# Attention remainders of the probabilities: from GpSimd and the vector engine together to the vector engine alone

## The reference, cut to what matters

```python
logits = q @ k.T * scale            # f32
p = softmax(logits, axis=-1)
out = p @ v
```

## Time and profile before

| | us |
|---|---|
| median of three runs (lowest, highest) | 4124.23 (4122.91, 4127.02) |
| span of the profiled execution, the only time the profile gives for itself | 4126.6 |
| attention, start of the first `ph` (line 1449) to start of the last, layer 0 | 388.81 to 932.48 |
| busy: PE, DVE, ACT, POOL | 3858.3, 1950.5, 1620.1, 1416.4 |

### The profile page before, as it was taken

How to read it: one execution, slowest core, us unless ns; L and a number is a source line. 1 busy time by engine, 2 the same in 40 slices (tenths; PEclk the granted TensorE clock), 3 DMA queues, 4 the chain that set the end, 5 groups by cost and what they waited for, 6 DMA issues and landing times. The chain is left out here.

```text
span 4126.6 us, 51789 instructions
## 1 busy us (share of the span) xinstructions
PE 3858.3 (93%) x19141; PEld 3134.3 (76%) x19141; DVE 1950.5 (47%) x2740; ACT 1620.1 (39%) x2581; POOL 1416.4 (34%) x904
## 2 busy tenths in 40 slices
PE   6899999998799999999869999999897999999997
PEld 5687787677588888888657767876675888888885
DVE  4114767871633343334450267678517343334336
ACT  2324767882422212221342357678624211221123
POOL 2223555662432212211432345556515112211224
PEclk8998999999899999999989989999998999999998
DMA  5321220101211111111123212111012111111113
GB/s 172 123 72 60 62 61 23 36 17 63 91 42 41 36 36 41 41 36 36 72 86 124 64 58 74 45 26 30 21 66 94 38 39 41 36 36 41 41 30 128
DMA packets 194303, 234.47 MB, mean 57 GB/s; under 512 B 13759, under 2 KB 157669, under 8 KB 193573
## 3 DMA queue, kind: packets, MB, share of 16 engines
q1 hardware_dynamic: 194125, 232.18, 18.3%
HBM read 178.05 MB, written 58.29 MB: 57 GB/s over the span
## 5 line engine op out<-in xcount | busy, mean ns | idle before, releaser
L211 PE MATMUL ps<-hh,wh 128*128 128x512 f32 (+1 forms) x3264 | 1180.8, 362 | 117.1 <-DVE wl L504 44.9
L212 PE MATMUL ps<-hl,wh 128*128 128x512 f32 (+1 forms) x3264 | 1165.1, 357 | 0.0
L213 PE MATMUL ps<-hh,wl 128*128 128x512 f32 (+1 forms) x3264 | 1162.7, 356 | 0.0
L211 PEld LDWEIGHTS ps<-hh,wh 128*128 128x128 f32 x3264 | 623.6, 191 | 216.6 <-issue 86.5
L1875 POOL TENSOR_TENSOR wl<-raw,wh 128x1024 fp32r<-128x1024 f32 x128 | 306.4, 2401 | 1279.4 <-ACT wh L1804 1279.4
L212 PEld LDWEIGHTS ps<-hl,wh 128*128 128x128 f32 x3264 | 623.6, 191 | 92.5 <-issue 5.7
L213 PEld LDWEIGHTS ps<-hh,wl 128*128 128x128 f32 x3264 | 622.6, 191 | 89.0
L1911 DVE SCALAR_TENSOR_TENSOR cb<-ps,params,cb 128x1023 f32<-128x1023 f32 (+1 forms) x176 | 147.3, 878 | 896.0 <-ACT cb L1813 896.0
L1549 DVE TENSOR_REDUCE mx<-ps 128x1 f32<-128x512 f32 x512 | 346.3, 685 | 219.5 <-PE ps L1352 116.1
L1526 POOL TENSOR_TENSOR pl<-p,ph 128x512 fp32r<-128x512 f32 (+1 forms) x244 | 311.9, 1279 | 367.3 <-ACT p L1450 357.5
L1449 ACT ACTIVATE ph<-ps 128x512 fp32r<-128x512 f32 (+1 forms) x576 | 331.6, 576 | 204.5 <-PE ps L1323 199.0
(11 more groups left out here) (167 smaller groups left out, 5443.5 us busy)
## 6 DMA issues: line engine op xcount, KB each, us to landing
raw<-in_w_up SPq DMA_DIRECT2D x88, 512.0 KB, 3.7
heads<-stage SPq DMA_DIRECT2D x38, 640.0 KB, 3.3
raw<-in_w_down SPq DMA_DIRECT2D x44, 512.0 KB, 3.6
xo<-residual SPq DMA_DIRECT2D x32, 640.0 KB, 6.3
rq<-heads SPq DMA_DIRECT2D x56, 320.0 KB, 3.9
raw<-in_w_in SPq DMA_DIRECT2D x32, 512.0 KB, 4.5
rk<-heads SPq DMA_DIRECT2D x32, 320.0 KB, 4.2
residual<-y SPq DMA_DIRECT2D x8, 1024.0 KB, 4.9
```

The source lines that it names most:

```text
L211: pe.matmul(out, wh, xh, start=(k == 0), stop=False)
L212: pe.matmul(out, wh, xl, start=False, stop=False)
L213: last = pe.matmul(out, wl, xh, start=False, stop=(k == len(pairs) - 1))
```

## The change

`pl_engine` returns "dve" for every step. Nothing else is edited, but three places follow from it: POOL's loop skips lines 1522 to 1527 in every step, DVE's loop has lines 1590 to 1595 in every step, and PE waits for `lo_dve` in every step. The wait for the order of two POOL instructions on different partitions (`settle`) sees fewer instructions.

```diff
     def pl_engine(g):
 
-        h, i = divmod(g, NS)
-        start = 0 if not new_kv(h + 1) else 7 if kind(h + 1) == "B" else 4
-        return "pool" if i >= start and i % 2 else "dve"
+        return "dve"
 
     def pl_count(g, who):
         return sum(pl_engine(x) == who for x in range(g + 1))
```

## The result

The changed kernel took 4139.82 us (median of 6 runs, 4138.47 to 4142.66) against 4125.87 us of the kernel before on the same chip (6 runs): a ratio of 1.0036 with a 95% interval of 1.0024 to 1.0047. It is 14 us slower. The forecast was 4126 with a range of 4110 to 4144; the time is in the range, beyond the likeliest case's own 4138. The walk had added up 2 us of the 14; the range holds the rest only because its upper end had been stretched towards a rival whose mechanism did not occur. That the time fell inside it is luck.

A forecast was written before the change was run, and what follows sets the result against it. PE, busy 93%, sets the time, and DVE counts only where PE waits for it. Terms of -1.1 +1.3 +1.6 +0.3 +0.35 -1.5 = +0.95 us a layer, +1.9 for both, on 4124.2 gave 4126; range 4110 to 4144.

The forecast's parts named there:

- likeliest case: Whole kernel: the place-by-place sum, 4126 us, with its own range 4115 to 4138; chance 0.65.
- C heads, step 15: Heads 8, 9, 10, 12, 13: earlier q splits and shorter holds turn the row 0.47 us earlier.
- C heads, step 7: Heads 8, 9, 10, 12, 13, 14: DVE's held remainder 5 precedes maximum 6; row 0.25 us later.
- Head 14: No q splits; remainder 13 waits for its `p`: +1.03 us at step 15, +0.25 at step 7, together +1.3.
- A heads: Heads 0, 1, 2: +0.4 us each at step 15; heads 1, 2: +0.2 each at step 7; together +1.6.
- B heads: Among heads 3 to 7: steps up to 6 unchanged, 14 us of room in a head; 0.
- Head 11: Like heads 8 to 10, but its values split takes the gain of step 15: +0.35 us.
- Heads 3 and 7: These two heads of a layer: +0.3 us together.
- End of the layer: PE's 1.54 us wait for POOL's remainder 15 disappears, DVE having it in time: -1.5 us a layer.
- faster, the collisions decide: Rival: remainders fall to 693 ns, `hh` to 0.42, half of PE's waits go: -18 us, 4106; chance 0.15.
- Slower, DVE becomes the engine: Rival: DVE never idle in steps 9 to 17 and 0 to 6 of heads 8 to 14; +18 us, 4142; chance 0.20.
- No measurable change: Rival: the work was hidden anyway, PE's waits stay; 4124 us, counted with the forecast's own case.

The follow-up runs named there:

- e3: Changed kernel plus six unused matmuls of 512 columns on PE ahead of the wait for step 7's row, heads 8 to 15: 4135.00 us, ratio 1.0018.
- e2: Changed kernel with the remainder of step 13 alone given back to GpSimd, all 16 heads: 4119.89 us, ratio 0.9981.
- e4: Changed kernel with `lo_output` replaced by a GpSimd memset of zeros that reads nothing from SBUF: 4113.95 us, ratio 0.9965.
- e5: Changed kernel with the remainders of steps 5 and 13 both given back to GpSimd: 4116.13 us, ratio 0.9974.
- e9: Kernel before, GpSimd keeping its 244 remainders, with DVE's own remainders taken one step later: 4107.65 us, ratio 0.9952.
- e8: Changed kernel with DVE's remainders one step later and `lo_output` waiting behind DVE's next remainder: 4113.13 us, ratio 0.9969.
- e10: Same kernel as e8, profiled and timed a second time: 4112.34 us, ratio 0.9964.
- e7: Changed kernel with DVE taking each remainder one step later, after the maximum: 4113.13 us, ratio 0.9970.

## Why the prediction was right and where it was wrong

The forecast put +0.95 us on a layer; attention grew by 6.6 (547.3 to 553.8 in layer 0, 547.1 to 553.8 in layer 1). The rest was 3.1 us shorter in the profiled executions, which is within what it varies by. Step by step, layer 0:

- *C heads, step 15*: forecast -0.47. Measured -0.47 in head 10, -0.48 in 12, -0.35 to -0.39 in 9 and 13. Right.
- *C heads, step 7*: forecast +0.25 as the position of the row. Measured +0.34 in head 12, +0.19 in 9 and 13. Right in heads 9, 12 and 13 (-0.15 to -0.21 a head for -0.22). **This is the step that failed in heads 8, 10 and 14**: there the head grew by some 1.9 us more at steps 7 and 8 than the kernel before has. The row was turned 11.30 us into head 10 and 11.30 into head 12, so no later; what the walk left out, and so put at nothing, is that a longer pause of PE can take TensorE to 1.2 GHz. e3 measured that term: 1.5 us a head, 4.5 a layer, 9 in all. That is two thirds of the 14 us.
- *Head 14*: forecast +1.3 with +1.03 at step 15, measured +1.02 there and, without the clock's 1.53, +1.40. The timeline shows `p` ready, the remainder of 256 columns, `hh` and the maximum behind it, against the earlier trace rows:

```profile
907.70 0.38 ACT L1448 ACTIVATE p<-ps 128x256 f32<-128x256 f32 x1
...
908.11 0.42 DVE L1592 TENSOR_TENSOR pl<-p,ph 128x256 fp32r<-128x256 f32 x1 [0.92 <-ACT p L1448]
...
909.16 0.42 DVE L1575 CAST hh<-ot 64x512 fp32r<-64x512 f32 x1
...
909.50 0.41 DVE L1549 TENSOR_REDUCE m<-ps 128x1 f32<-128x256 f32 x1
```

  The maximum starts 1.80 us after the start of that `p`; before it was 0.79. The 1.01 between them is the forecast's 1.03.
- *A heads*: forecast +1.6 for 0, 1 and 2, measured +0.20, +0.72, +0.60 in layer 0. The sum is right (1.5); head 0 was 0.25 us shorter at other steps, which the walk did not have. Against the earlier trace rows the same wait of remainder 13 for its `p`; e2 took 0.5 to 0.8 of it back.
- *B heads*: forecast 0, measured -0.05 to -0.01. Right, though the reason was half wrong: PE does wait for DVE there (e4), but for something that the change left alone.
- *Head 11*: +0.35 forecast, +0.66 measured, of it +0.76 at step 7. *Heads 3 and 7*: +0.3 forecast, +0.21 measured.
- *End of the layer*: -1.5 forecast, -0.7 measured. The remainder of step 15 is late on DVE as well, behind a `lo_output` of 1.79 us that starts at 935.98, where GpSimd's was 1.54 us late:

```profile
938.38 0.50 PE L1337 MATMUL ps<-pl,vh 128*128 128x512 f32 x1 [0.74 <-DVE pl L1592]
```

Leaving the clock out, the forecast of a layer was 0.95 and the measurement 6.6 - 4.5 = 2.1. The bounds of the likeliest case hold a slip: -9 to +12 around 4126 is 4117 to 4138, not 4115 to 4138; the measured time lies outside either.

Of the signs that the prediction names, GpSimd's busy time (1109 us for 1105) and the lengths of heads 9, 12 and 13 (29.8 us), of the A heads 1 and 2 and of the B heads came as said. DVE was busy for 2040 us, not 2080. Heads 8 and 10 lasted 31.4 us, over the 31 that was to show the forecast wrong, but with DVE busy for 26.45 of 31.37 us and not throughout, and the cause was the clock, not the order of `hl` and remainder 5, which the prediction gives for that case.

Of the rivals, "faster, the collisions decide" is refuted as put: the collisions fell (mean 808 ns for 971, `hh` 0.42 for 1.42), and the waits of PE ahead of a row rose. The rule of the Trainium skill ("SBUF — State Buffer", section "Who interferes with whom"), that a DVE instruction with two SBUF inputs contends with a GpSimd instruction that reads SBUF and not with one that only writes it, agrees with the traces (1.14 us beside `lo_output`, which reads; 0.67 in e4 with 0.32 us of a memset beside it). What such a hold costs depends on what stands behind the held instruction: at step 5 it is a maximum that PE waits for. "Slower, DVE becomes the engine" named the sign and nearly the size (4142) for a wrong reason: head 12 has the same DVE work as head 10 and got faster, and e5 gains 7.6 us a layer with seven of nine remainders on DVE. "No measurable change", which the prediction counts with its own case, is refuted as well: the interval of the ratio, 1.0024 to 1.0047, leaves out 1.

## What to carry to other kernels

Ask of a moved instruction not how long it takes but what is queued behind it, and what holds it: here one of nine places (step 5) and one more (step 13) cost more than the seven others gave back. Where a wait of PE is lengthened, even by 0.3 us, look at the granted clock of the stretch after it; the price of the pause may be several times the pause. And try the order within the queue before moving work to another engine: one step of lag, with the work divided as it was, gave 0.48% (e9), although head 11 lost by it.

## What was not expected of the hardware

- The same sequence of instructions with the same pause ran at 1.00 of the clock in head 12 and at 0.95 in head 10, the same in both layers. The pause alone is no sufficient reason; what else decides, its place in time perhaps, was not separated. Added matmuls without use (e3) took the falls away and made attention 3 us a layer shorter.
- A GpSimd memset that overlapped DVE's remainder for 0.32 us left it at 0.67 us (e4, head 10, 779.95); GpSimd's subtraction `lo_output` made remainder 5 last 1.14.
- Untouched phases differed by up to 8 us between kernels (3027.4 to 3035.3), and two of them by 3.6 and 4.1 us between two executions of one kernel (e8 and e10), which only their sum hides. A gain of 4.6 us a layer in attention (e8 over e7) did not show in the time.
